# Residual additions moved to GpSimd, row scalings kept on VectorE, eight normed blocks transposed by DMA, and the last output block written in halves

## The reference

```python
x = x + rmsnorm(merged @ w_out, g_mix_post)                # pooling and gated convolution, then w_out
x = x + rmsnorm(cross_attn(rmsnorm(x, g_x_pre), ...), g_x_post)
hid = jnp.square(jax.nn.relu(rmsnorm(x, g_ff_pre) @ w_up))
x = x + rmsnorm(hid @ w_down, g_ff_post)
```

## Time and profile before

| | us |
|---|---|
| median of 3 runs (lowest to highest) | 898.75 (897.88 to 900.32) |
| the profiled execution, its own time | 901.45 |
| its span on the slowest core (core 1) | 900.1 |
| spans of the 8 cores | 893.8 to 900.1 |
| PE busy | 859.5 |
| DVE busy / ACT busy / POOL busy | 448.9 / 432.4 / 53.0 |

### The profile page before, as it was taken

How to read it: one execution, slowest core, us unless ns; L and a number is a source line. 1 busy time by engine, 2 the same in 40 slices (tenths; PEclk the granted TensorE clock), 3 DMA queues, 4 the chain that set the end, 5 groups by cost and what they waited for, 6 DMA issues and landing times.

```text
span 900.1 us, 14693 instructions; the slowest of 8 cores (893.8 to 900.1 us)
## 1 busy us (share of the span) xinstructions
PE 859.5 (95%) x5018; PEld 453.0 (50%) x5018; DVE 448.9 (50%) x772; ACT 432.4 (48%) x1043; POOL 53.0 (6%) x66
## 2 busy tenths in 40 slices
PE   7898898999999999999999998999899999999996
PEld 4565444664456666544444443457454444444442
DVE  3788687476872222232142877886684222200133
ACT  4557888466873333332132386886684333200122
POOL 1100100000000000000001000000000000000000
PEclk9989989999999999999999999999999999999998
DMA  9997376719585654636829992171716746426022
GB/s 195 194 155 110 76 118 105 127 28 206 76 151 81 98 80 62 102 88 115 117 100 120 236 228 82 40 96 23 95 21 110 107 69 94 59 36 87 8 94 94
DMA packets 66793, 91.89 MB, mean 102 GB/s; under 512 B 2936, under 2 KB 58360, under 8 KB 66208
## 3 DMA queue, kind: packets, MB, share of 16 engines
q0 software_dynamic: 58080, 60.95, 48.1%
q1 hardware_dynamic: 8640, 30.00, 10.2%
HBM read 137.49 MB, written 12.30 MB: 166 GB/s over the span
## 4 chain that ended last, share of the span: by engine, by line
PE 80%; ACT 9%; issue 4%; DVE 4%; DMA 2%; ACTq 0%; DVEq 0%; SPq 0%; POOLq 0%
PE psum L393 77%; PE psum L397 3%; ACT stg L411 3%; ACT xsb L411 3%; ACT st L411 2%; ACT un L411 2%; DMA ring<-w_in 1%; DMA X<-xp 1%; DVE un L423 1%; DVE xT L414 1%; DMA conv_p<-stg 1%; DVE X L423 0%; DVE un L414 0%; DVE un L418 0%; DVE xsb L418 0%
## 5 line engine op out<-in xcount | busy, mean ns | idle before, releaser
L393 PE MATMUL psum<-xT,ring 128*128 128x352 bf16 (+6 forms) x2336 | 413.0, 333 | 3.6 <-DVE xT L414 2.5
L393 PEld LDWEIGHTS psum<-xT,ring 128*128 128x128 bf16 x2336 | 226.5, 98 | 167.5 <-issue 6.6
L393 PE MATMUL psum<-ring,un 128*128 128x512 bf16 (+1 forms) x1408 | 302.6, 380 | 0.0
L411 ACT ACTIVATE un<-psum 128x352 bf16<-128x352 f32 (+9 forms) x258 | 125.0, 492 | 201.2 <-PE psum L393 198.9
L393 PEld LDWEIGHTS psum<-ring,un 128*128 128x128 bf16 (+1 forms) x1408 | 130.7, 98 | 157.7 <-issue 9.1
L414 DVE TENSOR_TENSOR un<-un 128x352 bf16<-128x352 bf16 (+5 forms) x176 | 84.8, 483 | 156.8 <-ACT un L411 156.8
L414 DVE TENSOR_TENSOR stg<-psum,gp 128x1024 f32<-128x1024 f32 (+3 forms) x51 | 53.1, 1042 | 106.6 <-ACT stg L411 57.6
L411 ACT ACTIVATE stg<-psum 128x1024 bf16<-128x1024 f32 (+3 forms) x51 | 44.5, 873 | 104.8 <-PE psum L393 102.6
L414 DVE TENSOR_TENSOR xT<-psum,gcs 128x1024 bf16<-128x1024 bf16 (+2 forms) x52 | 60.0, 1155 | 35.7 <-PE psum L397 35.2
L393 PE MATMUL psum<-ring,mg 128*128 128x512 bf16 (+1 forms) x320 | 75.8, 388 | 0.0
L423 DVE SCALAR_TENSOR_TENSOR X<-stg,st,X 128x1024 f32<-128x1024 f32 (+3 forms) x51 | 56.3, 1104 | 6.8 <-DVE stg L414 4.7
(11 more groups left out here) (95 smaller groups left out, 517.1 us busy)
## 6 DMA issues: line engine op xcount, KB each, us to landing
ring<-w_up POOLq DMA_DIRECT2D x16, 1024.0 KB, 14.2
ring<-w_down POOLq DMA_DIRECT2D x16, 1024.0 KB, 10.7
X<-xp SPq DMA_DIRECT2D x16, 512.0 KB, 14.0
yp<-X SPq DMA_DIRECT2D x16, 512.0 KB, 2.7
ring<-w_in POOLq DMA_DIRECT2D x7, 1024.0 KB, 11.4
ring<-w_out POOLq DMA_DIRECT2D x4, 1024.0 KB, 31.8
ring<-w_q POOLq DMA_DIRECT2D x4, 1024.0 KB, 22.7
stg<-xp SPq DMA_DIRECT2D x8, 512.0 KB, 4.3
```

Source lines behind the costliest of these rows:

```text
L393: P.add("pe", lambda e: e.matmul(out, lhsT=lhsT, rhs=rhs, start=start, stop=stop), reads=[lhsT, rhs], writes=[out])
L411: P.add("act", lambda e: e.activation(out=out, in_=in_, func=func, scale=scale, **kw), reads=rd, writes=wr)
```

## The change

Four edits:

1. `out_block`: VectorE makes one instruction from PSUM, O = ps * rsqrt * gp into stg, where it made two. The addition of O to X is a `tensor_tensor` on GpSimd.
2. `out_block`, `p2`: the scaling of X into xsb is on VectorE for every block, the values of the second Square go to the junk area and no longer to xsb, and the transposes are due four ticks later where they were due three.
3. `hook0`: the scaled rows go from xsb to xT by a transposing DMA issued from SP, and the gain is multiplied in place in xT seven ticks later, where TensorE transposed into PSUM.
4. `down_evac`: the mean and eps of the first half are made at h = 0, so that at h = 1 the Ln takes the second half's sum directly, with the first half as bias, and the Identity goes. The last block's rows are written in two DMAs of 512 columns, the first from ScalarE's queue between the two additions.

```diff
-    def pre_a(Xap, r, key, on_act=False, xs=None):
+    def pre_a(Xap, r, key, on_act=False, xs=None, junk=None):
...
-        act(xs, Xap, AF.Square, accum=stat(key, 3, r))
+        act(xs if junk is None else junk, Xap, AF.Square, accum=stat(key, 3, r))
...
-        par = o_rr[0] % 2 == 0
...
-        tt(O, ps, gp[0:r, :], ALU.mult)
+        stt(O, ps, stat(key, 2, r), gp[0:r, :], ALU.mult, ALU.mult)
         xb = Xs(blk)
-        stt(xb, O, stat(key, 2, r), xb, ALU.mult, ALU.add)
+        P.add("pool", lambda e: e.tensor_tensor(out=xb, in0=xb, in1=O, op=ALU.add), reads=[xb, O], writes=[xb])
 
         def p2():
-            xs = pre_a(xb, r, key, par)
-            later(3, lambda: pre_b(xs, r, gi, xT3[:, :, c0 + 16:c0 + 16 + r]))
+            xs = pre_a(xb, r, key, False, None, junk)
+            later(4, lambda: pre_b(xs, r, gi, xT3[:, :, c0 + 16:c0 + 16 + r]))
...
         if h == 0:
             O = obuf(b)
             act(O, ps, AF.Square, accum=stat(key, 6, r))
+            act(stat(key, 6, r), stat(key, 6, r), AF.Identity, scale=1.0 / D, bias=epsb[0:r, 0:1])
...
-        act(stat(key, 0, r), stat(key, 6, r), AF.Identity, bias=stat(key, 7, r))
-        rstd(stat(key, 0, r), stat(key, 1, r), stat(key, 2, r), D)
+        act(stat(key, 1, r), stat(key, 7, r), AF.Ln, scale=1.0 / D, bias=stat(key, 6, r))
+        act(stat(key, 2, r), stat(key, 1, r), AF.Exp, scale=-0.5)
...
+            if last:
+                dma("act", yp[r0:r0 + 128, 0:512], xb[:, 0:512], wr=False)
             stt(xb[:, 512:1024], O, stat(key, 2, r), xb[:, 512:1024], ALU.mult, ALU.add)
...
+            elif last:
+                dma("sp", yp[r0:r0 + 128, 512:1024], xb[:, 512:1024], wr=False)
...
-            later(2, lambda: pre_b(xs, 128, 0, xT3[:, :, xcol(j):xcol(j) + 128]))
+            dst = xT3[:, :, xcol(j):xcol(j) + 128]
+            P.add("sp", lambda e: e.dma_start(out=dst, in_=xs, transpose=True), reads=[xs], writes=[dst], dma=True)
+            later(7, lambda: tt(dst, dst, gcs[:, 0:8].unsqueeze(2).to_broadcast([128, 8, 128]), ALU.mult))
```

3 lines of the change are left out of this document (2 added, 1 removed).

## The result

| | before | after |
|---|---|---|
| median (lowest to highest) | 899.12 us (897.88 to 900.32, 4 runs) | 908.69 us (907.67 to 909.48, 4 runs) |
| the profiled execution: span on the slowest core | 900.1 (core 1) | 906.3 (core 2) |
| spans of the 8 cores, their mean | 893.8 to 900.1, 896.7 | 902.5 to 906.3, 904.6 |

The change makes the kernel slower: ratio 1.0106, 95% interval 1.0087 to 1.0125, some 9.5 us. The forecast was 889.7, with a range of 885 to 904. (All times and ratios in this text leave out runs in which one half of the chip was disturbed.)

The account below looks back on a forecast made before the run. TensorE was taken as the bound, busy 859.5 of 900.1 us. Terms of -3.6 (transposing DMA), -0.7 (tail) and -4.8 (work by engine) summed to -9.1, giving 889.7 us against the median, range 885 to 904.

Parts of the forecast that it names:

- The step that failed: Output blocks: VectorE's scaling waits 0.8 us, 60% of GpSimd's remaining addition; cycle 3.8 against TensorE's 3.90.
- rival A: Output blocks: GpSimd's addition shuts out VectorE's scaling entirely; cycle 4.3 to 4.35 us, +8.5, less 4.3: 903; chance 0.27.
- The ends: Ends of output-block runs, where TensorE waits: forecast to fall from 11.5 to 6.7 us, -4.8.
- Loop S: Follow-up theory, not in the prediction: ScalarE's PSUM Square queues behind a Square awaiting the addition; some 3.8 us a block.
- by the three PSUM pairs: Inside output runs: the longer chain (multiply after rsqrt, addition 2.3 for 1.29 us) is covered by PSUM pairs and later transposes.
- V: Follow-up theory: GpSimd's addition shuts out VectorE's SBUF reads; the multiply, addition, scaling loop takes 4.29 us a block.
- The point from which it decides: Output blocks, full hold: a GpSimd addition over 1.9 us brings the cycle to TensorE's 3.9; at 2.5, 909.
- The 3.22 of the attention rows: Second group: TensorE's wait for attention weights queued on VectorE behind two output blocks' work; forecast to fall to 2.8 us.
- The convolution rows: Start of the mix outputs: VectorE rows reading two SBUF tiles while GpSimd adds; forecast to cost 1.0 us.
- C: Output blocks: no hold to speak of, or an addition near 1.3 us; -12.8, so 886; chance 0.15.
- D: stage_down: transposing DMA exceeds its cover of about 12 us, gains stall VectorE, the 3.6 is lost; 894 to 905; chance 0.07.
- B: Output blocks: partial hold, but addition of 2.6 us or more, or longer chain at ends; 894 to 899; chance 0.16.

Follow-up runs that it names:

- edits_3_and_4: Kernel before with the transposing DMA and both tail changes, its out_block as before; 896.61 us, ratio 0.9962.
- shared_512: Changed kernel with the addition shared: GpSimd adds the first 512 columns, VectorE the other 512; 898.70 us, ratio 0.9987.
- half_the_columns: Changed kernel with GpSimd adding only the first 512 columns, the other 512 of O left out of X; 892.27 us, ratio 0.9914.
- split_add: Changed kernel with GpSimd's addition made in two instructions of 512 columns; 908.11 us, ratio 1.0092.
- half_on_scalar: Changed kernel with every second scaling back on ScalarE as a Copy, additions still on GpSimd; 915.98 us, ratio 1.0206.
- edit1_only: Kernel before with only the single VectorE multiply and the addition on GpSimd; every second scaling stays on ScalarE; 922.69 us, ratio 1.0259.
- tail_only: Kernel before with the tail alone changed: Identity moved to h = 0, last block's rows written in two halves; 897.94 us, ratio 0.9986.
- transpose_and_fold: Kernel before with the transposing DMA and no Identity at h = 1, last block written in one DMA; 896.66 us, ratio 0.9959.

## Why the prediction was wrong

**The step that failed** is "the scaling waits for GpSimd, for some 60% of the overlap ... 60% of it, 0.8, is waited. Cycle: ... 3.8 us against TensorE's 3.90. It holds, narrowly". Measured: where a scaling runs into an addition, it ends 0.54 to 0.56 after the addition's end (core 2), so it waits for all that is left of it; 2.04 where 1.5 was forecast, cycle 4.29, as rival A has it. (The last block of a run, with no addition beside its scaling, takes 0.74 to 0.76.)

The rows from before did not say otherwise; they were misread. The scaling of 1.11 ended at 254.71 + 1.11 = 255.82, 0.50 after GpSimd's DMA issue had ended (255.32). A scaling takes 0.75 by itself, and only some 0.5 of that comes after the end of a hold, so its delay is the overlap less 0.25, and not a share of the overlap. A second place of the same trace (core 1) tells the two readings apart:

```profile
20.62 0.74 POOL L1189 DMA_DIRECT2D wpool<-w_pool  x1 [15.20 <-DMA X<-xp]
20.95 0.91 DVE L418 TENSOR_SCALAR un<-X,st 128x1024 bf16<-128x1024 f32 x1 [4.59 <-ACT st L411]
```

The overlap is 0.41 and the delay 0.16, which is 39% of it; but the end is again 0.50 after the issue's. Beside the addition 0.55 comes after it, so the delay is the overlap less 0.2. By that the forecast's own 1.3 of overlap gives a wait of 1.1 and a cycle of 4.1, above the 3.90 of TensorE. The overlap was 1.50 (249.65 to 251.15) and the wait 1.29.

I cited it and gave it 0.27.

**The size.** Edits 1 and 2 cost (1.0106 - 0.9962) x 899 = 12.9 us against edits_3_and_4; rival A had +8.5, and with it the 904 that ended the range. Its loss inside the runs was not too small: it had 0.4 for each of 34 blocks, and in the last run TensorE's packets come 3.90 apart (658.26, 662.16, 666.07) all the same. What it lacked:
- The ends. It put the loss inside the runs in place of the waits at the ends, and these stayed: the nine long waits for xsb alone are 11.0 us. My forecast had them shrink by 5. Where the loop is under 3.90 (shared_512) edits 1 and 2 still cost 0.0025 x 899 = 2.2. Only with the shorter chain of half_the_columns do the ends give something.
- Loop S is not part of the 12.9, as far as the rows show: in the changed kernel its rsqrt is ready 1.1 early. But the chain's length was treated as covered "by the three PSUM pairs", and it is not covered in general: ScalarE takes its instructions in order, and the Square of X, which waits for the addition, stands ahead of the PSUM Square that the block after next needs. At some 3.8 us a block against V's 4.29 it takes over as soon as V is loosened (split_add) or the Copy is in it (half_on_scalar; edit1_only fits).

**The sensitivity had the right direction.** "The point from which it decides: an addition over 1.9 us with a full hold": at 2.37 the kernel loses 9.5, at 1.30 (half_the_columns) edits 1 and 2 give -4.3. No run lies near 1.9 itself. GpSimd's duration (2.3 forecast, 2.37 measured) was right, too. With the right duration and the wrong hold the sign of the sum was wrong.

**The other terms.**
- Edit 3: -3.6 forecast. TensorE's stage got 4.1 shorter, 0.52 a packet where I had 0.45; the DMAs landed in 8.2 us in the median. One took 12.9, over the 12 that I had named as a sign of being wrong, and VectorE waited 16.7 us for them in all and ScalarE 19.7, but TensorE did not wait; on the other side the end of the program is 1.4 longer. Net -2.7; measured 0.0033 x 899 = -3.0, so two errors nearly cancel.
- Edit 4: -0.7 forecast; Identity -0.4, split write -0.3 to -0.5: right. tail_only measured -1.3, with an interval of -0.3 to -2.2.
- The 3.22 of the attention rows, forecast at 2.8: 3.52, since the scaling ahead of them was held for 2.65, and 0.44 more for the rows that are held themselves (2.05 for 0.48). The convolution rows with two SBUF operands cost VectorE 2.1 more in each group, 4.2 in sum, where I had 1.0 for TensorE's time.
- C did not occur: there is a hold. Of D one transposing DMA was over its bound, without a wait of TensorE. B's longer chain at the ends is there: 2.2 in shared_512.

**What beats both kernels** with nothing left out is edits_3_and_4 or transpose_and_fold, 896.6 to 896.7 against 899.1 and 908.7, a gain of 0.4%: the transposing DMA and the tail, and no arithmetic on GpSimd.

## What to carry to other kernels

Before work moves to GpSimd, list what VectorE has to read from SBUF (not from PSUM) while it runs, and add the whole rest of GpSimd's instruction (here less some 0.2 us) to each of these: the busy share (GpSimd 15%, VectorE 52%) says nothing about it. Price a moved instruction in every loop that goes through it, one for each engine whose queue is in order; here a second loop, some 0.5 shorter, took over when the first was loosened, so that the experiment on the first alone looked as if it were not the cause. And read a hold by when the held instruction ends, not by how much longer it took: two rows with different overlaps tell a fixed rest after the hold from a share of the overlap.
